# Weighting the expert rows on their way out of PSUM and adding them up in DRAM by the scatter, in a mixture-of-experts layer on one Trainium2 core

## The chip, the core and the metric

The kernel runs on one core of a Trainium2 chip. A core has a matrix engine (TensorE, PE in the profile), a vector engine (VectorE, DVE), an activation engine (ScalarE, ACT), a general one (GpSimd, POOL) and a sync engine (SyncE, SP) that here only issues transfers. Transfers run on 16 DMA engines, fed by queues; those that SP issues and those that POOL issues go through queues of their own. SBUF is the on-chip memory, PSUM the small memory into which TensorE writes, DRAM the device memory. The metric is the time of one launch in microseconds (us); less is better.

## The reference: what is computed

The input is 1024 latent tokens of 1024 float32 numbers and 256 context tokens. One layer is computed: modulation, input projection, two kinds of attention, output projection, and then the part that matters here, 32 experts of which each token takes four. Cut to that part:

```python
logits = t @ w_router + b_router
top_val, top_idx = lax.top_k(logits, TOP_K)        # TOP_K = 4
top_w = jax.nn.softmax(top_val, axis=-1)
# rows sorted by expert, in blocks of 128 with one expert each; empty places have weight 0
def expert_block(idx, e):
    hu = t[idx] @ w1[e] + b1[e]                    # 1024 -> 2048
    glu = jnp.minimum(hu[:, 0::2], 7.0)
    lin = jnp.clip(hu[:, 1::2], -7.0, 7.0)
    act = glu * jax.nn.sigmoid(1.702 * glu) * (lin + 1)
    return act @ w2[e] + b2[e]                     # 1024 -> 1024
y = y_rows * row_w[:, None]
out = jax.ops.segment_sum(y, row_tok, num_segments=1024)
x = x + ga2 * rmsnorm(out, g_post_ffn)
```

## The kernel before, in words

The program has five stages, each a block with a barrier behind it: `front` (modulation and projections), `attention`, `middle` (output projection, router, table of slots), `experts` and `combine`. Each engine has its own instruction list in each stage, written by hand, and they wait for each other by semaphores. Nothing reorders them.

**Attention** begins with transfers. SP loads `w_out` (two of 2 MB) into the ring, then a mask for head group A (`mask_a`), the bias of group B (two of 1.25 MB) and its mask (`mask_b`). POOL loads `sink` and copies the first queries (`queries`, L557). VectorE's first score needs `mask_a` and `sink` (L712). POOL adds `mask_b` to the bias (L570), and the heads of group B need the sum (`bias_ready`).

**Middle** ends with the router on VectorE: it picks four experts a token, computes `K.weights` (L995) and, for each of the 4096 choices, a slot number `K.slots`. Then POOL scatters 4096 records of two integers into `slot_d` (L855), 32 scatters. A record is (token, row of `y_d`), where choice k of a token has row `1024 k + token`. `slot_d` was filled in `front` with records of empty slots: token 0 and one of 128 spare rows of `y_d`.

**Experts** works in steps (`program`, L1146). A step is one expert with one block (single, R=1) or two blocks (pair, R=2) of 128 rows. The first loop runs a single step and a pair step alternately, 16 times each; the second runs 3 single steps. Together 35 steps and 51 blocks. A step has six units of weights, each 2 MB: four up (`UP`) and two down (`DOWN`). For each unit SP loads it into a ring of three (L1163), when VectorE and POOL have split the unit three before it (`lo_done`, `pool_lo_done`); ScalarE rounds it to its high part (L1256), VectorE (L1312, seven eighths) and POOL (L1208, one eighth, k = 7) form the low part, and TensorE does three products of each pair of tiles (L1402 to L1404).

POOL's list in a step (L1215 to L1243) also carries the rows:

- it copies the row numbers out of `record` to `y_row` (L1219), waits for that, and loads the next step's records (L1186);
- it splits unit 2, waits for the records, and gathers the next step's rows from `h2_d` into `xg` (L1190), one gather a block;
- it splits units 3, 4, 5 and the next step's 0;
- when ScalarE has copied the last result to `y` (L1296), it scatters `y` to `y_d` (L1239), one scatter a block, splits the next step's unit 1, and waits until the scatters have landed (L1242) before the next step begins.

TensorE transposes the gathered rows (`rows`, L1382) after its up units, and then the last activations (`columns`, L1389), before its down units.

**Combine** takes tiles of 128 tokens, eight in all. SP loads the four rows of each token (`yg`, 2 MB a tile) and the residual (`x1`, 0.5 MB), with two tiles of `yg` at a time; VectorE multiplies and adds the four rows (L1502, L1504), ScalarE takes the mean square (L1492), VectorE finishes (L1512 to L1516), and POOL stores the tile (L1483).

## Time and profile before

| | us |
|---|---|
| median of 3 runs | 3386.89 |
| lowest and highest of them | 3383.48, 3387.11 |
| the profiled execution's own time | 3385.55 |
| its span, first to last instruction | 3383.9 |

| engine | busy, us | share of the span |
|---|---|---|
| TensorE | 2891.7 | 85% |
| VectorE | 1887.1 | 56% |
| ScalarE | 1407.9 | 42% |
| GpSimd | 866.9 | 26% |

The stages lie one behind the other. The trace has the first instruction of `attention` at 453.0 us, the first of `experts` at 1262.1, and the first of `combine` at 3299.4, so `experts` is 60% of the span and `combine` 84.5 us. The DMA engines moved 629.36 MB, 444 MB of it expert weights. Busy time is an average over stages with different limits; the shares above do not say what bounds a stage.

### The profile page before, as it was taken

What the parts mean: (1) busy time and instruction counts of PE and PEld (TensorE: products, weight loads), DVE (VectorE), ACT (ScalarE), POOL (GpSimd) and SP (SyncE); (2) the same over time, 40 slices, a digit from 0 to 9 for tenths busy, and PEclk for the clock granted to TensorE, in tenths of its full rate; (3) what the DMA queues carried; (4) which work ended last, traced back from release to release, by engine and by line L of the source; (5) the groups of instructions that cost most, each with busy time, mean ns of one, the idle gap of its engine ahead of it and who ended that gap; (6) DMA issues with size and microseconds to landing.
All of it is one profiled execution on the core that took longest, in us unless ns stands there. A gap on an engine that the chain in (4) does not pass through costs nothing. (4 is left out here: it accounts for less than half of the span.)

```text
span 3383.9 us, 40318 instructions
## 1 busy us (share of the span) xinstructions
PE 2891.7 (85%) x13206; PEld 2182.2 (64%) x13207; DVE 1887.1 (56%) x2864; ACT 1407.9 (42%) x1667; POOL 866.9 (26%) x609
## 2 busy tenths in 40 slices
PE   4899989999957707999999999999999999999980
PEld 0254667777734406787787778777777777777760
DVE  0430024444422246767767776766677677767786
ACT  0100025555511105545545554555455445445551
POOL 1000021312111153223322422333233333323330
PEclk8999989999978858999999999999999999999995
DMA  9700032213132108667666765776676577667678
GB/s 242 254 25 25 13 93 68 68 45 86 45 105 87 62 18 306 239 217 260 238 221 242 269 232 211 263 269 213 234 261 247 207 265 254 229 219 276 241 281 310
DMA packets 285165, 629.36 MB, mean 186 GB/s; under 512 B 9922, under 2 KB 11202, under 8 KB 284962
## 3 DMA queue, kind: packets, MB, share of 16 engines
q1 hardware_dynamic: 261558, 549.12, 47.3%
q0 software_dynamic: 23568, 79.73, 6.6%
q8 instruction: 23, 0.38, 0.0%
q14 instruction: 16, 0.13, 0.0%
HBM read 584.63 MB, written 50.26 MB: 188 GB/s over the span
## 5 line engine op out<-in xcount | busy, mean ns | idle before, releaser
L1312 DVE TENSOR_TENSOR w_lo_x<-wring_x,w_hi_x 128x2048 fp32r<-128x2048 f32 (+1 forms) x422 | 874.0, 2115 | 195.8 <-PE psum L1404 191.5
L1256 ACT ACTIVATE w_hi_x<-wring_x 128x2048 fp32r<-128x2048 f32 x424 | 787.4, 1907 | 102.1 <-DMA wring_x<-in_w_mlp 101.8
L1402 PE MATMUL psum<-w_hi_x,x_hi_x 128*128 128x512 f32 x1632 | 676.6, 415 | 5.6 <-DVE w_lo_x L1312 5.6
L1403 PE MATMUL psum<-w_lo_x,x_hi_x 128*128 128x512 f32 x1632 | 637.2, 390 | 0.0
L1404 PE MATMUL psum<-w_hi_x,x_lo_x 128*128 128x512 f32 x1632 | 637.1, 390 | 0.0
L1208 POOL TENSOR_TENSOR w_lo_x<-wring_x,w_hi_x 128x512 fp32r<-128x512 f32 x212 | 327.8, 1550 | 888.3 <-PE psum L1404 810.5
L1402 PE MATMUL psum<-w_hi_x,a_hi_x 128*128 128x512 f32 x816 | 353.5, 433 | 0.0
L1402 PEld LDWEIGHTS psum<-w_hi_x,x_hi_x 128*128 128x128 f32 x1632 | 308.4, 189 | 65.9 <-DVE w_lo_x L1312 6.5
L1404 PEld LDWEIGHTS psum<-w_hi_x,x_lo_x 128*128 128x128 f32 x1632 | 306.9, 188 | 65.8
L1403 PEld LDWEIGHTS psum<-w_lo_x,x_hi_x 128*128 128x128 f32 x1632 | 307.6, 188 | 62.1
L1403 PE MATMUL psum<-w_lo_x,a_hi_x 128*128 128x512 f32 x816 | 329.9, 404 | 0.0
L1404 PE MATMUL psum<-w_hi_x,a_lo_x 128*128 128x512 f32 x816 | 327.6, 401 | 0.0
L1285 ACT ACTIVATE sig_x<-glu_x 128x256 f32<-128x256 f32 x204 | 84.9, 416 | 532.3 <-DVE glu_x L1356 532.1
L1356 DVE TENSOR_SCALAR glu_x<-psum 128x256 f32<-128x256 f32 x204 | 85.7, 420 | 270.5 <-PE psum L1404 270.2
L654 ACT ACTIVATE S<-S,negm 128x896 f32<-128x896 f32 (+1 forms) x128 | 119.6, 934 | 207.4 <-DVE negm L717 113.5
L465 PE MATMUL psum<-hT,ring 128*128 128x512 f32 (+1 forms) x496 | 200.9, 564 | 5.2 <-DVE hT L381 4.6
L630 PE MATMUL psum<-v,PT 128*128 (+1 forms) x1536 | 187.2, 273 | 0.0
L630 PEld LDWEIGHTS psum<-v,PT 128*128 128x128 f32 x1536 | 183.8, 194 | 0.0
L1404 PEld LDWEIGHTS psum<-w_hi_x,a_lo_x 128*128 128x128 f32 x816 | 160.7, 197 | 35.8
L1402 PEld LDWEIGHTS psum<-w_hi_x,a_hi_x 128*128 128x128 f32 x816 | 162.4, 199 | 32.9
L1403 PEld LDWEIGHTS psum<-w_lo_x,a_hi_x 128*128 128x128 f32 x816 | 161.6, 198 | 34.2
L1204 POOL TENSOR_TENSOR poolgate_x<-poolgate_x 128x1 f32<-128x1 f32 x70 | 96.0, 1372 | 341.7 <-ACT y_x L1296 246.0
(249 smaller groups left out, 3549.0 us busy)
## 6 DMA issues: line engine op xcount, KB each, us to landing
wring_x<-in_w_mlp SPq DMA_DIRECT2D x212, 2048.0 KB, 8.0
ring<-in_w_ada SPq DMA_DIRECT2D x12, 2048.0 KB, 9.0
bias<-bias_d SPq DMA_DIRECT2D x16, 1280.0 KB, 14.2
yg<-y_d SPq DMA_DIRECT2D x8, 2048.0 KB, 10.4
ring<-in_w_in SPq DMA_DIRECT2D x4, 2048.0 KB, 9.0
xin<-in_x SPq DMA_DIRECT2D x8, 512.0 KB, 5.1
ring<-in_w_out SPq DMA_DIRECT2D x2, 2048.0 KB
mix_d<-o SPq DMA_DIRECT2D x8, 512.0 KB, 6.6
```

Of the source, the lines that this page charges most:

```text
L465: last = pe.matmul(ps[:, g % 4, 0:width], lhs, rhs, start=(k == 0), stop=(k == KD - 1))
L630: last = pe.matmul(ps[:, 6 + s // NHA, head * HD:(head + 1) * HD], PT[:, s % 2, c * P:(c + 1) * P], v, start=(c == 0), stop=(c == chunks - 1))
L654: act.activation(S[:, s % 2, 0:keys(s)], S[:, s % 2, 0:keys(s)], ACT.Exp, bias=negm[:, s:s + 1], accum_out=den[:, s:s + 1]).then_inc(p_don ...
L1204: pool.tensor_tensor(poolgate[:, 1:2], poolgate[:, 0:1], poolgate[:, 0:1], ALU.add).then_inc(gate_open, 1)
L1208: pool.tensor_tensor(w_lo[:, n % LO, KP:, :], ring[:, n % RING, KP:, :], w_hi[:, n % HI, KP:, :].bitcast(F32), ALU.subtract).then_inc(pool ...
L1256: act.activation(w_hi[:, n % HI, k, :], ring[:, n % RING, k, :], ACT.Copy).then_inc(hi_done, 1)
L1285: act.activation(sig[:, j % 2, :], glu[:, j % 2, :], ACT.Sigmoid, scale=ALPHA).then_inc(sig_done, 1)
L1312: dve.tensor_tensor(w_lo[:, n % LO, k, :], ring[:, n % RING, k, :], w_hi[:, n % HI, k, :].bitcast(F32), ALU.subtract).then_inc(lo_done, 1)
L1356: dve.tensor_scalar(glu[:, s, :], pairs[:, :, 0], LIMIT, None, ALU.min).then_inc(glu_done, 1)
L1402: pe.matmul(bank, hi[:, r, k, :], w_hi[:, n % HI, k, :], start=False, stop=False)
L1403: pe.matmul(bank, hi[:, r, k, :], w_lo[:, n % LO, k, :], start=False, stop=False)
L1404: last = pe.matmul(bank, lo[:, r, k, :], w_hi[:, n % HI, k, :], start=False, stop=(k == KD - 1))
```

## The change

1. `y_d` has one row a token (1024) and 128 spare rows in place of 4096 and 128. Both it and 128 new spare rows of `h2_d` are filled with zeros by two transfers that POOL issues at the start of `attention`; POOL waits for them at that stage's end.
2. A record is now (token, weight as float32 bits). Four copies on VectorE put the weights into the records. Empty slots have a spare row as token and weight 0, so the gather of an empty slot reads a spare row of zeros in place of row 0.
3. In a step POOL copies the weights of the block to `y_weight` beside `y_row`, and the semaphore `gate_open` counts four a step in place of three. ScalarE's copy out of PSUM takes `y_weight` as its scale, and waits for it once a step.
4. The scatter adds: `compute_op=ALU.add`. Its row number is the token.
5. `combine` loads one row a token straight into `acc` (0.5 MB a tile), and the residual beside it, with three tiles in flight and buffers for all eight. The four multiplications and additions are gone.

```diff
-    record = np.stack(np.broadcast_arrays(token, token + SEQ * np.arange(TOPK)[None, :, None]), axis=-1)
+    record = np.stack([token, 0 * token], axis=-1)
...
-    spare = TOPK * SEQ + np.arange(SLOTS) % P
-    out["k_empty"] = np.stack([0 * spare, spare], axis=-1).astype(np.int32)
+    spare = SEQ + np.arange(SLOTS) % P
+    out["k_empty"] = np.stack([spare, 0 * spare], axis=-1).astype(np.int32)
...
-            self.h2_d = dram("h2_d", (SEQ, D))
+            self.h2_d = dram("h2_d", (SEQ + P, D))
...
-            self.y_d = dram("y_d", (TOPK * SEQ + P, D))
+            self.y_d = dram("y_d", (SEQ + P, D))
...
             pool.dma_start(sink[:, :], io["sink_a"].to_broadcast([P, NHA])).then_inc(sink_loaded, 16)
+            pool.dma_start(K.y_d, io["k_zeros"][0:1, 0:D].to_broadcast([SEQ + P, D])).then_inc(sums_zeroed, 16)
+            pool.dma_start(K.h2_d[SEQ:SEQ + P, :], io["k_zeros"][0:1, 0:D].to_broadcast([P, D])).then_inc(sums_zeroed, 16)
...
             pool.wait_ge(sink_loaded, 16)
+            pool.wait_ge(sums_zeroed, 32)
...
+            for k in range(TOPK):
+                link(dve.tensor_copy(record[:, k, :, 1].bitcast(F32), K.weights[:, :, k]))
...
-                pool.tensor_tensor(y_row[:, 0:st.R], record[:, 0:st.R, 1], int_zero[:, 0:st.R], ALU.add).then_inc(gate_open, 1)
-                pool.wait_ge(gate_open, 3 * st.passes + 3)
+                pool.tensor_tensor(y_row[:, 0:st.R], record[:, 0:st.R, 0], int_zero[:, 0:st.R], ALU.add).then_inc(gate_open, 1)
+                pool.tensor_copy(y_weight[:, 0:st.R], record[:, 0:st.R, 1].bitcast(F32)).then_inc(gate_open, 1)
+                pool.wait_ge(gate_open, 4 * st.passes + 4)
...
-                    pool.indirect_dma_start(K.y_d, bass.IndirectOffsetOnAxis(ap=y_row[:, r:r + 1], axis=0), y[:, r, :], None).then_inc(y_stored, 16)
+                    pool.indirect_dma_start(K.y_d, bass.IndirectOffsetOnAxis(ap=y_row[:, r:r + 1], axis=0), y[:, r, :], None, compute_op=ALU.add).then_inc(y_stored, 16)
...
+                        act.wait_ge(gate_open, 4 * st.passes + 4)
...
-                        act.activation(y[:, r, h * UNIT:(h + 1) * UNIT], ps[:, 4 + (h * st.R + r) % 2, :], ACT.Copy).then_inc(y_copied, 1)
+                        act.activation(y[:, r, h * UNIT:(h + 1) * UNIT], ps[:, 4 + (h * st.R + r) % 2, :], ACT.Copy, scale=y_weight[:, r:r + 1]).then_inc(y_copied, 1)
...
-                if t >= 2:
-
-                    sp.wait_ge(acc_done, t - 1)
-                sp.dma_start(yg[:, t % 2, :, :], y_rows[t]).then_inc(tile_loaded[t % 2], 16)
...
+                s = t % INFLIGHT
+                if t >= INFLIGHT:
+                    sp.wait_ge(tile_loaded[s], 32 * (t // INFLIGHT))
+                sp.dma_start(acc[:, t, :], K.y_d[t * P:(t + 1) * P, :]).then_inc(tile_loaded[s], 16)
+                sp.dma_start(x1[:, t, :], K.x1_d[t * P:(t + 1) * P, :]).then_inc(tile_loaded[s], 16)
```

Three places show how the instructions now stand. In the rows a bracket names the semaphores that an instruction waits for, and the numbers are the shape. First POOL at the start of `attention`, before and then after; `sink`, `y_d` and `h_d` are targets of transfers.

```order
L546 MEMSET zeros 128x256
L547 MEMSET qz 128x2048
L548 DMA sink<-in_sink_a 128x8
L557 COPY qz<-qaT 64x512 [waits tiles_loaded,zeros_set]
L557 COPY qz<-qaT 64x512
```

```order
L546 MEMSET zeros 128x256
L547 MEMSET qz 128x2048
L548 DMA sink<-in_sink_a 128x8
L549 DMA y_d<-in_k_zeros 1152x1024
L550 DMA h2_d<-in_k_zeros 128x1024
L559 COPY qz<-qaT 64x512 [waits tiles_loaded,zeros_set]
L559 COPY qz<-qaT 64x512
```

Two transfers of 1152 and 128 rows of 4 KB now stand between `sink` and the first queries. Second, POOL at the end of a pair step and the start of the single step behind it, before and after (`y_stored` counts landed scatters; the rows behind the line of dots are the start of the single step, which the loop runs next; unnamed rows, ISA and REGISTER_ALU, set registers or carry a wait).

```order
L1204 TENSOR_TENSOR poolgate_x<-poolgate_x 128x1 [waits y_copied_x]
L1239 DMA y_d<-y_x,y_row_x 4224x1024 x2
L1240 REGISTER_ALU
L1207 ISA [waits prod_done_x]
L1208 TENSOR_TENSOR w_lo_x<-wring_x,w_hi_x 128x512 [waits hi_done_x]
L1242 REGISTER_ALU
...
L1219 TENSOR_TENSOR y_row_x<-record_x,int_zero_x 128x1 [waits gate_open_x]
L1220 REGISTER_ALU
L1186 ISA [waits gate_open_x]
L1186 DMA record_x<-slot_d 128x2x2
```

```order
L1210 TENSOR_TENSOR poolgate_x<-poolgate_x 128x1 [waits y_copied_x]
L1246 DMA y_d<-y_x,y_row_x 1152x1024 x2
L1247 REGISTER_ALU
L1213 ISA [waits prod_done_x]
L1214 TENSOR_TENSOR w_lo_x<-wring_x,w_hi_x 128x512 [waits hi_done_x]
L1249 REGISTER_ALU
...
L1225 TENSOR_TENSOR y_row_x<-record_x,int_zero_x 128x1 [waits gate_open_x]
L1226 COPY y_weight_x<-record_x 128x1
L1227 REGISTER_ALU
L1192 ISA [waits gate_open_x]
L1192 DMA record_x<-slot_d 128x2x2
```

The order is the same; one copy stands ahead of the load of the records, and the two scatters now add. Third, SP in `combine`, first two tiles and the first that waits, before and after.

```order
L1470 DMA yg<-y_d 128x4x1024
L1474 DMA x1_rows<-x1_d 128x1024
L1470 DMA yg<-y_d 128x4x1024
L1474 DMA x1_rows<-x1_d 128x1024
L1470 DMA yg<-y_d 128x4x1024 [waits acc_done]
```

```order
L1476 DMA acc<-y_d 128x1024
L1477 DMA x1_rows<-x1_d 128x1024
L1476 DMA acc<-y_d 128x1024
L1477 DMA x1_rows<-x1_d 128x1024
L1476 DMA acc<-y_d 128x1024
L1477 DMA x1_rows<-x1_d 128x1024
L1476 DMA acc<-y_d 128x1024 [waits tile_loaded5_0]
```

The loads are a quarter of the size, and from the fourth tile on they wait for an earlier load in place of VectorE.

## Rows read from the trace of the kernel before

**Rows 1.** The page: busy time, share of the span, instructions of TensorE.

```profile
PE 2891.7 (85%) x13206; PEld 2182.2 (64%) x13207; DVE 1887.1 (56%) x2864; ACT 1407.9 (42%) x1667; POOL 866.9 (26%) x609
```

**Rows 2.** Last stage by window: stretch, length, busy times, TensorE clock, DMA share, GB/s.

```profile
3299.40:3369.40 70.00, 0.00 (x0) 0.00 (x0) 48.88 (x48) 11.39 (x22) 4.89 (x8) 0.50 0.96 359
```

**Rows 3.** Timeline, end of experts and last stage: start, length, engine, line [idle before].

```profile
3292.35 1.00 POOL L1239 DMA_INDIRECT y_d<-y_x,y_row_x  x1
...
3299.43 0.37 SPq L1470 DMA_DIRECT2D yg<-y_d  x1
...
3374.14 1.06 ACT L1492 ACTIVATE squares<-acc 128x1024 f32<-128x1024 f32 x1 [8.43 <-DVE acc L1504]
...
3379.71 0.53 POOL L1483 DMA_DIRECT2D out<-out_rows  x1 [2.12 <-DVE out_rows L1516]
```

**Rows 4.** Windows at the start of attention, columns as in rows 2.

```profile
453.00:463.00 10.00, 4.63 (x8) 2.52 (x8) 0.23 (x1) 1.28 (x1) 5.03 (x7) 0.66 0.78 220
463.00:470.70 7.70, 0.00 (x0) 0.00 (x0) 0.31 (x2) 0.00 (x0) 0.00 (x0) 0.63 1.06 363
470.70:483.30 12.60, 10.45 (x50) 8.59 (x51) 5.91 (x23) 5.25 (x11) 0.14 (x1) 0.68 0.95 198
```

**Rows 5.** Timeline at the start of attention: VectorE's first score, POOL's bias.

```profile
470.70 0.06 DVE L710 MEMSET gate<- 128x1 f32 x1 [7.33 <-DMA mask_a<-in_k_mask_a]
...
483.17 11.04 POOL L570 TENSOR_TENSOR bias<-bias,mask_b 128x5120 f32<-128x5120 f32 x1 [24.86 <-DMA mask_b<-in_k_mask_b]
```

**Rows 6.** DMA issues: the zero fill that front has, KB, us to landing.

```profile
skew_d<-in_k_zeros POOLq DMA_DIRECT2D x1, 2914.0 KB, 15.7
```

**Rows 7.** Timeline of VectorE in the router: a copy of 128x8 and the next.

```profile
1191.35 0.17 DVE L1015 COPY scan<-scan 128x8 f32<-128x8 f32 x1
1191.55 0.22 DVE L1016 TENSOR_TENSOR scan<-scan 128x56 f32<-128x56 f32 x1
```

**Rows 8.** Timeline of POOL from a pair step's scatters into a single step.

```profile
1996.22 2.33 POOL L1239 DMA_INDIRECT y_d<-y_x,y_row_x  x1 [0.16 <-issue]
1998.85 0.97 POOL L1239 DMA_INDIRECT y_d<-y_x,y_row_x  x1 [0.30 <-issue]
...
2002.94 1.22 POOL L1219 TENSOR_TENSOR y_row_x<-record_x,int_zero_x 128x1 int32<-128x1 int32 x1 [1.78 <-DMA y_d<-y_x,y_row_x]
2004.85 0.79 POOL L1186 DMA_DIRECT2D record_x<-slot_d  x1 [0.70 <-POOL y_row_x L1219]
...
2013.13 0.96 POOL L1190 DMA_INDIRECT xg_x<-h_d,record_x  x1 [0.30 <-issue]
2014.10 2.57 POOL L1208 TENSOR_TENSOR w_lo_x<-wring_x,w_hi_x 128x512 fp32r<-128x512 f32 x2
```

**Rows 9.** Timeline of TensorE: transposes of gathered rows (L1382), of last activations (L1389).

```profile
2018.69 1.09 PE L1382 MATMUL psum<-ident,xg_x 128*128 128x128 f32 x8 [1.24 <-DMA xg_x<-h_d,record_x]
2023.86 0.69 PE L1389 MATMUL psum<-ident,act_o_x 128*128 128x128 f32 x2 [4.08 <-DVE act_o_x L1361]
...
2252.84 1.10 PE L1382 MATMUL psum<-ident,xg_x 128*128 128x128 f32 x8 [1.67 <-DMA xg_x<-h_d,record_x]
...
2256.58 0.44 PE L1389 MATMUL psum<-ident,act_o_x 128*128 128x128 f32 x2 [2.64 <-DVE act_o_x L1361]
```

**Rows 10.** Windows of 1 us behind the two scatters, columns as in rows 2.

```profile
1999.00:2000.00 1.00, 1.00 (x6) 0.78 (x5) 0.73 (x2) 0.98 (x2) 0.98 (x2) 1.00 0.91 369
2000.00:2001.00 1.00, 1.00 (x6) 0.83 (x5) 0.97 (x2) 0.99 (x3) 1.00 (x1) 1.00 0.84 332
2001.00:2002.00 1.00, 1.00 (x6) 0.84 (x5) 0.97 (x3) 1.00 (x1) 0.15 (x1) 1.00 0.87 348
```

**Rows 11.** One line's instructions (L1219): ns min/median/max, first and last start.

```profile
L1219 POOL TENSOR_TENSOR y_row_x<-record_x,int_zero_x x35: 197/390/1699, 1288.9 to 3259.3; 128x1 int32<-128x1 int32 x19, 128x2 int32<-128x2 int32 x16
```

More of the change, by code:

```diff
@@ L1106, in experts @@
         record, y_row, int_zero = sb("record", [P, RMAX, 2], I32), sb("y_row", [P, RMAX], I32), sb("int_zero", [P, RMAX], I32)
+        y_weight = sb("y_weight", [P, RMAX])
         poolgate = sb("poolgate", [P, 2])
@@ L1457, in combine @@
         rows_loaded = sem("rows_loaded5")
-        tile_loaded = [sem("tile_loaded5_0"), sem("tile_loaded5_1")]
+        INFLIGHT = 3
+        tile_loaded = [sem(f"tile_loaded5_{t}") for t in range(INFLIGHT)]
         stored = [sem("stored5_0"), sem("stored5_1")]
-        acc_done, rms_done, out_done, dve_own, act_own = sem("acc_done"), sem("rms_done5"), sem("out_done"), sem("dve_own5"), sem("act_own5")
-        y_rows = K.y_d[0:TOPK * SEQ, :].rearrange("(k t p) d -> t p k d", t=T, p=P)
+        rms_done, out_done, dve_own, act_own = sem("rms_done5"), sem("out_done"), sem("dve_own5"), sem("act_own5")
         block = ctx.enter_context(nc.Block())
@@ L1497, in _ @@
             link = linker(dve, dve_own)
-            def add(t):
-                s = t % 2
-                dve.wait_ge(tile_loaded[s], 32 * (t // 2 + 1))
-                link(dve.tensor_scalar(acc[:, s, :], yg[:, s, 0, :], K.weights[:, t, 0:1], None, ALU.mult))
-                for k in range(1, TOPK):
-                    ins = dve.scalar_tensor_tensor(acc[:, s, :], yg[:, s, k, :], K.weights[:, t, k:k + 1], acc[:, s, :], ALU.mult, ALU.add)
-                    if k + 1 < TOPK:
-                        link(ins)
-                ins.then_inc(acc_done, 1)
-            def finish(t):
+            dve.wait_ge(rows_loaded, 32)
+            link(dve.tensor_tensor(gate2[:, :], gate2[:, :], gain[:, :], ALU.mult))
+            for t in range(T):
                 s = t % 2
```

33 lines of the change are left out of this document (11 added, 22 removed).

## The prediction, made before the changed kernel ran

> **What bounds the kernel now.** I read the page first, then windows of the three stages that the change touches, then the timeline of each. TensorE is busy 85% of the span [rows 1], nearly all of it in `experts`; that share says nothing of the other stages, so each is read by itself.
>
> The last stage is bound by transfers. Over its first 70 us the DMA engines are 0.96 busy at 359 GB/s, while VectorE works 48.88 of 70 us [rows 2]. The stage lasts from SP's first load at 3299.43 to the end of the span at 3383.9 [rows 3], 84.5 us.
>
> The start of `attention` is bound by transfers too. The DMA share is 0.78, 1.06 and 0.95 in the three stretches up to 483.3 [rows 4]. VectorE's first score waits for `mask_a` until 470.70, and POOL's addition to the bias waits for `mask_b` until 483.17 [rows 5]. The bias is not early: the addition ends at 494.2, about when the first head of group B comes up.
>
> In `experts` a pair step is TensorE's own: each weight unit serves two blocks and everything else has time. The single step behind a pair is the tight place, and there are 16 of them. There POOL's list is a chain: scatters, their landing, `y_row`, load of the records, gathers, splits [rows 8]. TensorE wants the gathered rows 1.24 us before they are there; they are transposed from 2018.69 on, and then TensorE stands for 4.08 us until 2023.86 for the last activations, which come from VectorE [rows 9]. So the chain on POOL is late already, but something else is later. The eight transposes take about 2.15 us, so the slack of the chain there is 2023.86 - 2018.69 - 2.15 = 3.0 us. The other step shown has 2256.58 - 2252.84 - 2.15 = 1.6. I formed it for all sixteen: 1.6 to 3.6, mean 2.84. This number decides the case.
>
> **The change part by part.**
>
> *The last stage.* It reads 8 x 0.524 MB of sums and as much of residual, 8.39 MB in place of 20.97, plus 1.05 MB for `gate2` and its gain as before. Work on VectorE falls to a reciprocal, a product and an addition a tile, below the time of a tile's transfers, and nothing waits for it. The last tile lands when the reads and about five of the eight stored tiles (2.62 MB) are through: 12.06 MB at 359 GB/s, the mean that includes the stage's start [rows 2], is 33.6 us. From the last square to the end of the span it is 3383.9 - 3374.14 = 9.8 us [rows 3]. Together 43.4, a gain of 41.1 us. Bounds: no store moves before the last tile lands (26.3 + 9.8 = 36.1, a gain of 48), or all do (38.0 + 9.8 = 47.8, a gain of 37).
>
> *The zero fill.* 1280 rows of 4 KB, 5.24 MB, start at about 456 us, in the stretch where the engines are full. SP's queue and POOL's share them, so both `mask_a` and `mask_b` get later; the fill ends before `mask_b` lands. At 363 GB/s [rows 4] the fill takes 14.4 us, and I take all of it as delay: after 483 the engines are idle, but the wait is over by then. Bounds: 0, if the fill is served behind SP's loads; 27.6, if it goes at the 190 GB/s of the other fill from the same zeros, 2.98 MB in 15.7 us [rows 6], and nothing beside it. That one shared the engines with weight loads, so I keep to 14.4. The two issues ahead of the first queries (about 0.6 us each) are hidden behind the wait for `mask_a`; without that cover they would cost 1.2.
>
> *Four copies in the router*, on the path to POOL's slot scatters. A linked copy of 128x8 takes 0.20 us start to start [rows 7]: +0.8.
>
> *ScalarE's scale and its wait.* A scale from a column in place of a constant; the wait is for a POOL instruction at the step's beginning, four units earlier. Nothing, hidden by those units; nobody waits behind it unless POOL's chain is 20 us late.
>
> *The adding scatter.* No row of before shows one. Two plain ones move 1.05 MB in the three windows from 1999 to 2002, and the share of the engines adds up to 0.91 + 0.84 + 0.87 = 2.6 us [rows 10]. Each row of `y_d` must now be read before it is written, so the engines read twice as much. I take the engine time doubled, +2.6 us at the second scatter's landing. Bounds: 0 (the reads from DRAM run beside those from SBUF), and +5.2 or more if a row is read, added and written without overlap. For the issue on POOL, 0.97 us free and 2.33 where it began beside VectorE [rows 8], I take +0.3 (0 to 1).
>
> A rule weighs on this term. The Trainium skill, Collectives: The Full Stack, section "The bandwidth ceiling: the fold count and why AG ≠ RS ≠ AR", says that an addition inside the DMA engines costs no cycles by itself but needs two source reads through one ring, so that the rate halves (it gives 1.93). No row here shows it; by it the sum would be the same as mine, since it names the doubling that I took as the middle.
>
> *`y_weight` on POOL.* It stands between `y_row` and the load of the records. `y_row` itself takes 0.197 us at least [rows 11], and 1.22 in the single step, where VectorE is splitting [rows 8]. I take 0.7, bounds 0.2 and 1.2. The 0.70 us between an instruction's end and the load that waits for it stays once.
>
> *The sum on the chain.* 2.6 + 0.3 + 0.7 = 3.6 us later in each single step behind a pair. Queued behind it on POOL are the record load, the split of unit 2, the gathers, the splits of 3 and 4. TensorE waits for the splits of 2 and 3 (the second comes 0.3 us before it is needed) and then for the gather, but the product of unit 3 is needed only at VectorE's next piece at about 2022, so a stall there is inside the slack. What is late next is the gathered rows: 3.6 - 2.84 = 0.76 us, sixteen times, 12.2 us. Bounds of the delay: 0.2 (no cost) to 7.4 (4.6 each, 73 us). The two single steps behind singles have one scatter, a delay of 1.3 + 0.3 + 0.7 = 2.3, below their slack of 2.6 and more: nothing. Pair steps have 11 us a unit: nothing.
>
> *The last scatter* has nobody to hide it: half of 2.6, +1.3, ahead of the barrier.
>
> *The sum*: -41.1 + 14.4 + 0.8 + 12.2 + 1.3 = -12.4 us. The profiled execution took 3385.55; the median of the runs is 1.3 above it, and I count from the median: 3374.5.
>
> **The rivals.**
>
> *Rival 1, the addition is free.* The chain gets 1 us later and stays under its slack. Then -41.1 + 14.4 + 0.8 = -25.9: 3361. For it: the engines are idle before 1999, and reads from DRAM and from SBUF come from different places. Against: both pass the same 16 engines, and 0.87 of them is taken while a scatter runs [rows 10].
>
> *Rival 2, the scatter's landing becomes the bound of the single steps.* Place: the wait for `y_stored` ahead of `y_row`. If the engine time grows by 5.2, the issue by 0.6 and the copy costs 1.2, the delay is 7.0, the cost 4.2 x 16 = 67 us, with 2.6 for the last scatter: -41.1 + 14.4 + 0.8 + 67 + 2.6 = +43.7: 3431. It turns the sign once the cost per step passes 24.6 / 16 = 1.5 us, a delay of 4.4, which is only 0.8 above my middle. For it: the weight load that SP issues at 2001.4 shares the engines with the second half of the scatters, and a stall of TensorE can lower its clock; in the first stretch of `attention` the granted clock is 0.66 [rows 4]. Against: up to 3 us are hidden in every step.
>
> *Rival 3, the fill goes at 190 GB/s* and holds up the loads for 27.6 us: +13.2 on the forecast, 3388, no change to be measured.
>
> **How the numbers follow.** Forecast 0.38, own range 3362 to 3388 (delay 3.0 to 4.6, stage gain 37 to 48); rival 1 0.22; rival 2 0.25, from 3394 up; rival 3 0.10; the rest, 0.05, a cost that I have not seen, on the slow side. The range that should hold it 8 times in 10 is 3358 to 3425. A difference of 0.2% (6.8 us) is about what a measurement of this kernel can tell from none. Faster by more: all of rival 1 and two thirds of the forecast, 0.46. Within: the rest of the forecast and half of rival 3, 0.20. Slower: 0.34.
>
> **What would show it.** The last stage 43 us long with the engines about full; the first score of `attention` at 482 to 485 and the bias at 497; windows behind two scatters with about 5.2 us of engine time; `y_row` 2.9 us later behind the scatters; TensorE's wait for the gathered rows about 5 in place of 1.2 us, and that for the last activations near 1. I am wrong if the landing moves by over 3.7 us, if the issue of an adding scatter takes much longer on POOL, or if the fill does not delay `mask_b`.

## The result, and the profile of the changed kernel

The changed kernel is slower. Its median is 3418.84 us (four runs, 3412.23 to 3421.43) against 3385.18 us for the kernel before; the ratio is 1.0108 with a 95% interval of 1.0082 to 1.0133, and the two medians lie 34 us apart. The prediction said 3374.5, faster by 11. The time lies inside the predicted range, and the sign is wrong.

The profiled execution took 3421.43 us, its span is 3419.6. Cut at the first load of records in `experts` and at SP's first load of the last stage, the two profiled spans compare like this:

| stretch | before | after | difference | predicted |
|---|---|---|---|---|
| up to `experts` | 1262.1 | 1287.3 | +25.2 | +15.2 |
| `experts` | 2037.3 | 2086.7 | +49.4 | +13.5 |
| last stage | 84.5 | 45.6 | -38.9 | -41.1 |
| span | 3383.9 | 3419.6 | +35.7 | -12.4 |

The gain came as forecast. Both costs came out larger, and the one in `experts` nearly four times as large.

**Attention.** These are the timeline rows that answer to [rows 5], and the fill's own row (KB, us from issue to landing):

```profile
492.24 0.06 DVE L713 MEMSET gate<- 128x1 f32 x1 [29.38 <-DMA mask_a<-in_k_mask_a]
...
505.77 11.05 POOL L572 TENSOR_TENSOR bias<-bias,mask_b 128x5120 f32<-128x5120 f32 x1 [46.00 <-DMA mask_b<-in_k_mask_b]
```

```profile
y_d<-in_k_zeros POOLq DMA_DIRECT2D x1, 4608.0 KB, 32.0
```

The first score starts 21.5 us later and the bias 22.6 us later. (The start of the bias differs by some us from one execution to the next: 500.9 to 506.0 us in the five traces with the fill at this place, 480.1 to 485.6 in the six of kernels without a fill.) The windows of the same stretch, columns as in [rows 2], show what the engines did meanwhile:

```profile
453.00:463.00 10.00, 4.26 (x8) 2.47 (x8) 0.54 (x2) 1.28 (x1) 6.32 (x9) 0.66 0.73 235
463.00:473.00 10.00, 0.00 (x0) 0.00 (x0) 0.00 (x0) 0.00 (x0) 0.00 (x0) 0.63 1.02 289
473.00:483.00 10.00, 0.00 (x0) 0.00 (x0) 0.00 (x0) 0.00 (x0) 0.00 (x0) 0.50 1.02 264
483.00:493.00 10.00, 0.00 (x0) 0.00 (x0) 0.76 (x2) 0.00 (x0) 0.00 (x0) 0.50 1.02 252
```

The engines are full, share 1.02, at 252 to 289 GB/s, where the loads alone ran at 363 [rows 4].

**Experts.** These rows are the same transition as [rows 8], the first two of [rows 9] and [rows 10], from a pair step's scatters into the single step behind it. The step's first product starts at 2029.7 here, and at 1993.4 before. First POOL, then SP and ScalarE, then TensorE:

```profile
2032.57 2.96 POOL L1246 DMA_INDIRECT y_d<-y_x,y_row_x  x1 [0.16 <-issue]
2035.84 1.56 POOL L1246 DMA_INDIRECT y_d<-y_x,y_row_x  x1 [0.30 <-issue]
2036.86 1.88 POOL L1214 TENSOR_TENSOR w_lo_x<-wring_x,w_hi_x 128x512 fp32r<-128x512 f32 x1
2043.31 0.19 POOL L1225 TENSOR_TENSOR y_row_x<-record_x,int_zero_x 128x1 int32<-128x1 int32 x1 [4.57 <-DMA y_d<-y_x,y_row_x]
2043.44 0.18 POOL L1226 COPY y_weight_x<-record_x 128x1 f32<-128x1 f32 x1
2044.34 0.81 POOL L1192 DMA_DIRECT2D record_x<-slot_d  x1 [0.72 <-POOL y_weight_x L1226]
```

```profile
2038.96 0.37 SPq L1169 DMA_DIRECT2D wring_x<-in_w_mlp  x1
```

```profile
2049.08 3.72 ACT L1263 ACTIVATE w_hi_x<-wring_x 128x2048 fp32r<-128x2048 f32 x2 [4.66 <-DMA wring_x<-in_w_mlp]
2052.70 0.40 ACT L1292 ACTIVATE sig_x<-glu_x 128x256 f32<-128x256 f32 x1
```

```profile
2058.01 1.09 PE L1390 MATMUL psum<-ident,xg_x 128*128 128x128 f32 x8 [1.88 <-DMA xg_x<-h_d,record_x]
2061.76 0.69 PE L1397 MATMUL psum<-ident,act_o_x 128*128 128x128 f32 x2 [2.65 <-DVE act_o_x L1369]
```

The second scatter's start to `y_row` takes 7.47 us, before it was 4.09 [rows 8]. Counted from the step's first product, the gathered rows are transposed at 28.3 us in place of 25.3. TensorE's wait in front of them has hardly grown, 1.88 for 1.24 us [rows 9]; over all sixteen steps the mean is 1.8 for 1.2. But the last activations, which I had taken to stand still, have moved too, from 30.5 to 32.0, and TensorE still stands for them when the rows are transposed: 2.65 us here and 2.8 on average, before 4.08 and 3.8. In none of the sixteen steps is this second wait shorter than 2.0 us, so the gathered rows never come last.

What the prediction did not look at is ScalarE. The same row of before, and the weight load behind it, are:

```profile
2001.37 0.37 SPq L1163 DMA_DIRECT2D wring_x<-in_w_mlp  x1
```

```profile
2009.69 3.72 ACT L1256 ACTIVATE w_hi_x<-wring_x 128x2048 fp32r<-128x2048 f32 x2 [2.86 <-DMA wring_x<-in_w_mlp]
```

This is the load of unit 4, the first `down` unit. SP issues it when its ring slot is free, that is, when POOL has split unit 1, and that split stands behind the two scatters on POOL. Before, it was issued 8.0 us into the step and was there at 16.3; after, 9.2 and 19.3. Behind its conversion ScalarE has the sigmoid of unit 2's activations; VectorE's product waits for that sigmoid, VectorE's split of unit 4 is queued behind the product, and behind the split come the activations of unit 3, for which TensorE waits. These are the three rows of VectorE, before and after: that product, the split of unit 4, and the first operation on unit 3's result.

```profile
2013.82 3.14 DVE L1361 TENSOR_TENSOR act_o_x<-lin_x,sig_x 128x256 f32<-128x256 f32 x1 [0.77 <-ACT sig_x L1285]
...
2017.21 5.01 DVE L1312 TENSOR_TENSOR w_lo_x<-wring_x,w_hi_x 128x2048 fp32r<-128x2048 f32 x2
2022.15 0.41 DVE L1356 TENSOR_SCALAR glu_x<-psum 128x256 f32<-128x256 f32 x1
```

```profile
2053.20 2.43 DVE L1369 TENSOR_TENSOR act_o_x<-lin_x,sig_x 128x256 f32<-128x256 f32 x1 [1.79 <-ACT sig_x L1292]
...
2055.89 3.94 DVE L1320 TENSOR_TENSOR w_lo_x<-wring_x,w_hi_x 128x2048 fp32r<-128x2048 f32 x2
2059.76 0.41 DVE L1364 TENSOR_SCALAR glu_x<-psum 128x256 f32<-128x256 f32 x1
```

The page's row for ScalarE's conversions tells the same of the whole span; these are the rows of before and of after, idle time before them last:

```profile
L1256 ACT ACTIVATE w_hi_x<-wring_x 128x2048 fp32r<-128x2048 f32 x424 | 787.4, 1907 | 102.1 <-DMA wring_x<-in_w_mlp 101.8
```

```profile
L1263 ACT ACTIVATE w_hi_x<-wring_x 128x2048 fp32r<-128x2048 f32 x424 | 787.3, 1907 | 156.1 <-DMA wring_x<-in_w_mlp 155.8
```

ScalarE waits 54 us more for weights. By the timelines of the sixteen single steps 2.1 us of it a step lie in front of unit 4 and 0.8 in front of unit 5. The windows behind the scatters show why the load lands late. Two scatters are 1.05 MB, as in [rows 10], but now they keep the engines full for twice as long, at about half the rate (the last two windows hold the beginning of the weight load too):

```profile
2036.00:2037.00 1.00, 1.00 (x6) 0.83 (x5) 0.97 (x3) 0.99 (x2) 1.00 (x2) 1.00 1.21 115
2037.00:2038.00 1.00, 1.00 (x6) 0.81 (x6) 1.00 (x1) 1.00 (x2) 1.00 (x2) 1.00 0.85 152
2038.00:2039.00 1.00, 1.00 (x6) 0.84 (x5) 1.00 (x1) 1.00 (x1) 0.74 (x1) 1.00 1.07 213
2039.00:2040.00 1.00, 1.00 (x7) 0.81 (x6) 0.97 (x3) 1.00 (x2) 0.00 (x0) 1.00 1.04 164
2040.00:2041.00 1.00, 1.00 (x6) 0.84 (x5) 1.00 (x1) 1.00 (x1) 0.00 (x0) 1.00 1.05 188
```

**The last stage**, as one window, and the wait that VectorE had in it:

```profile
3374.00:3404.00 30.00, 0.00 (x0) 0.00 (x0) 11.72 (x14) 12.68 (x25) 3.30 (x6) 0.50 0.98 381
3404.00:3419.60 15.60, 0.00 (x0) 0.00 (x0) 10.26 (x11) 0.15 (x1) 2.13 (x4) 0.50 0.35 142
```

```profile
3384.65 1.23 DVE L1502 TENSOR_TENSOR gate<-gate,gain 128x1024 f32<-128x1024 f32 x1 [23.17 <-DMA gain<-in_g_post_ffn]
```

The loads are through after 30 us, faster than I had reckoned. A tail of 15.6 us follows: VectorE could not start on the first tile until `gain` was there, 10.6 us into the stage, and then met stores that still held its two buffers (waits of 4.92, 2.46 and 0.55 us).

### The profile page after: what moved, and what is told of

It is laid out like the page before. It is cut to its first block and busy times, and to the rows that moved or that the text cites. A ratio compares the mean times of both kernels' runs of the same rounds, so it can differ in the third digit from the quotient of the medians.

```text
span 3419.6 us, 40371 instructions
## 1 busy us (share of the span) xinstructions
PE 2920.2 (85%) x13206; PEld 2187.4 (64%) x13207; DVE 1882.7 (55%) x2836; ACT 1417.0 (41%) x1667; POOL 866.8 (25%) x646
## 5 line engine op out<-in xcount | busy, mean ns | idle before, releaser
L1320 DVE TENSOR_TENSOR w_lo_x<-wring_x,w_hi_x 128x2048 fp32r<-128x2048 f32 (+1 forms) x422 | 883.0, 2136 | 194.6 <-PE psum L1412 190.8
L1214 POOL TENSOR_TENSOR w_lo_x<-wring_x,w_hi_x 128x512 fp32r<-128x512 f32 x212 | 351.6, 1663 | 888.0 <-PE psum L1412 782.3
## 6 DMA issues: line engine op xcount, KB each, us to landing
bias<-bias_d SPq DMA_DIRECT2D x16, 1280.0 KB, 14.1
```

What stands on the lines that cost most here:

```text
L1214: pool.tensor_tensor(w_lo[:, n % LO, KP:, :], ring[:, n % RING, KP:, :], w_hi[:, n % HI, KP:, :].bitcast(F32), ALU.subtract).then_inc(pool ...
L1320: dve.tensor_tensor(w_lo[:, n % LO, k, :], ring[:, n % RING, k, :], w_hi[:, n % HI, k, :].bitcast(F32), ALU.subtract).then_inc(lo_done, 1)
```

## The experiments

All were compared with the kernel before in the same session. Theory W is the one from the trace above: the late load of unit 4, through ScalarE and VectorE, sets the length of the single step. Rival L is the prediction's chain: landing, `y_row`, records, gather. The table at the end of this section has the steps side by side.

**e1, plain scatters.**

```diff
-  ... y[:, r, :], None, compute_op=ALU.add).then_inc(y_stored, 16)
+  ... y[:, r, :], None).then_inc(y_stored, 16)
```

> The changed kernel with plain scatters in place of adding ones: a row of the result holds one expert's part and not the sum, all else stays (the weight on leaving PSUM, the fill, the short last stage). The changed kernel takes 3418.8 us; its stage experts is 49.4 us longer than before. Theory (the addition itself makes experts longer: longer issue on POOL, later landing, more load on the DMA engines): nearly all of the 49 us comes back, what remains is the copy of the weight (0.2 us a step) and the later scale; experts within 4 us of before, about 3370 to 3374. Rival (the copy of the weight, the wait on ScalarE and the scale from a column, 689 in place of 600 ns, hold up the step): at least 15 us of the 49 stay, 3385 or more.

Measured: 3371.54 us, ratio 0.9977 (0.9967 to 0.9987). `experts` and the last stage together take 2085.0 us of the profiled span, 47.3 less than in the changed kernel. The single step is at 44.86 us, before 44.99. So the addition itself makes 47 of the 49 us, and the weight on leaving PSUM (689 in place of 600 ns an operation), its wait and the copy on POOL cost nothing that can be seen.

**e2, the fills behind SP's first loads.**

```diff
             load(0)
+            sp.dma_start(K.y_d, ...to_broadcast([SEQ + P, D])).then_inc(sums_zeroed, 16)
+            sp.dma_start(K.h2_d[SEQ:SEQ + P, :], ...).then_inc(sums_zeroed, 16)
             with sp.Fori(0, T - 1) as i:
```

> The changed kernel with the two zero fills issued by SP behind its first loads of attention (masks and bias of tile 0) in place of POOL ahead of them. Theory (the fill costs what it takes from these loads): POOL's first addition to the bias starts at 483 again in place of 505.8, the stage is 22.6 us shorter, about 3396. Rival (the fill costs the same wherever it runs in this stage, because the load of mask and bias of tile 1 then comes late in its place): VectorE waits for the second tile's mask, 3410 or more.

Measured: 3387.60 us, ratio 1.0028 (1.0013 to 1.0042). By the two ratios that is 27 us below the changed kernel; their intervals leave room for 22.6. The timeline has the bias where it was before the change:

```profile
481.93 11.06 POOL L573 TENSOR_TENSOR bias<-bias,mask_b 128x5120 f32<-128x5120 f32 x1 [24.98 <-DMA mask_b<-in_k_mask_b]
```

The fill itself takes longer there, 36.6 us to landing, and nobody waits for it. The bytes are the same; what cost was their place ahead of the loads that the stage waits for. (The edit also moves the fills from POOL's queue to SP's, and no run separates the place from the queue.)

**e3, POOL's split of unit 1 ahead of the scatters.**

```diff
+                pool.wait_ge(prod_done, units_done(st, NU))
+                split(unit + NU + 1, 1)
                 pool.wait_ge(y_copied, DOWN * (st.blocks + st.R) + 2)
                 gate()
                 (scatters)
-                pool.wait_ge(prod_done, units_done(st, NU))
-                split(unit + NU + 1, 1)
```

> The changed kernel with POOL's part of the split of the next step's unit 1 issued ahead of the scatters in place of behind them. Theory W (the single step is held up by the weight load of unit 4, which waits for this split and shares the DMA engines with the scatters): the load of unit 4 is issued 2 to 3 us earlier, ScalarE's wait for it falls from 4.6 to 2.5 us or less, and 1 to 2.7 us come back in each of 16 single steps: 3376 to 3403. Rival L (the single step is held up by the landing of the scatters, y_row, the records and the gather, as I predicted): the scatters start about 1 us later, so each of 16 single steps gets up to 1 us longer: 3419 to 3435.

Measured: 3527.30 us, ratio 1.0449 (1.0431 to 1.0466), by the two ratios 115 us above the changed kernel. Both theories missed it. In the same transition as above (first product at 2050.2):

```profile
2057.73 1.56 POOL L1248 DMA_INDIRECT y_d<-y_x,y_row_x  x1 [0.30 <-issue]
2069.87 0.18 POOL L1225 TENSOR_TENSOR y_row_x<-record_x,int_zero_x 128x1 int32<-128x1 int32 x1 [10.58 <-DMA y_d<-y_x,y_row_x]
...
2071.72 1.28 POOL L1214 TENSOR_TENSOR w_lo_x<-wring_x,w_hi_x 128x512 fp32r<-128x512 f32 x1
```

```profile
2073.06 0.79 PE L1410 MATMUL psum<-w_hi_x,x_hi_x 128*128 128x512 f32 x1 [6.08 <-POOL w_lo_x L1214]
```

The load of unit 4 was issued 5.6 us into the step, 3.6 earlier, as W said, and was still there only at 18.8. The scatters begin 2.8 us later than in the changed kernel, since POOL's split now stands ahead of them. With the load beside them from the start, the second one took 12.1 us from its start to `y_row` in place of 7.5. POOL's split of unit 2 is queued behind that wait, and TensorE stands 6 us for it inside unit 2's product. Whichever goes first, the load and the two adding scatters are both through only at about 19 us into the step. Behind the scatters hang POOL's splits, and they have little room too.

**e4, the landing off the chain.** The single step gets its own column of `y_row`, and POOL waits for `y_stored` behind the next gathers.

```diff
+                ycol = 0 if st.R == 2 else 2
-                pool.tensor_tensor(y_row[:, 0:st.R], ...
+                pool.tensor_tensor(y_row[:, ycol:ycol + st.R], ...
...
                 gather(next_r)
+                pool.wait_ge(y_stored, 16 * st.blocks + 16)
+                pool.sem_inc(y_free, 1)
...
-                pool.wait_ge(y_stored, 16 * (st.blocks + st.R))
-                pool.sem_inc(y_free, 1)
```

(An unused small load raises `y_stored` by 16 once at the start; the single steps behind singles keep their old wait.)

> The changed kernel with a column of y_row for the single step apart from the pair's, so that POOL waits for the landing of the scatters only behind the next gathers in place of ahead of y_row. Rival L (the landing is on the chain that holds up TensorE): the delay of about 3.4 us leaves the chain, and the 2.7 us a step come back: about 3375, or less. Theory W (the weight load of unit 4 holds it up): records and gathers come 5 us or more earlier and TensorE's wait for the gathered rows vanishes, but its wait for the last activations stays as long; the time changes by less than 10 us, 3409 to 3422.

Measured: 3409.49 us, ratio 1.0099 (1.0082 to 1.0116), where the changed kernel has 1.0108: not told apart. The mean single step is 0.7 us shorter. In this transition (first product at 2023.8) the load of the records is issued 10.2 us into the step in place of 14.6 and the first gather at 17.0 in place of 20.8. The issue is as early again as before the change (mean of the first gather 17.7, before 17.3). The rows themselves are not: they are transposed at 27.4 us on average, in the changed kernel at 28.3, before at 25.1, since the gathers now run beside the weight loads. ScalarE's conversion of unit 4 stays late, at 19.2:

```profile
2040.76 2.79 POOL L1196 DMA_INDIRECT xg_x<-h_d,record_x  x1 [0.52 <-issue]
```

```profile
2042.98 3.72 ACT L1266 ACTIVATE w_hi_x<-wring_x 128x2048 fp32r<-128x2048 f32 x2 [3.40 <-DMA wring_x<-in_w_mlp]
```

L said that 2.7 us a step come back, and TensorE would stop waiting for the rows; neither came. By itself this run leaves open what rows as early as before would have given. That they are not what costs follows with the wait behind them: in each of the sixteen steps, here as in the changed kernel, TensorE stands for the last activations after the rows are transposed (2.9 us on average, 1.8 at least).

**e5 and e6, bytes that nobody waits for, in the kernel before.** After e3 a broader theory stood beside W: the engines are full in that stretch, and each byte in it is paid (theory D). SP loads 1.05 MB more into a buffer of its own, behind unit 4's load, in each single step (e5) or in each pair step (e6).

```diff
                     load(st, n, e)
+                    if n == 4 and st.R == 1 and st.s is st.p:       # e6: st.R == 2
+                        sp.dma_start(extra[:, :, :], K.x1_d[0:2 * P, :]...).then_inc(extra_loaded, 16)
```

> The kernel before, with one more transfer that nobody uses: in each single step of the first loop SP loads 256 rows of x1_d (1.05 MB) into a buffer of its own, behind the weight load of unit 4; POOL's list is untouched. In the trace the DMA engines are full from 8 us behind the start of a single step (the first weight load) to 36 us. Theory D (the single step behind a pair is bound by the engine time of all transfers in that stretch, so the adding scatter costs what it takes from the engines and not what its landing delays): 1.05 MB at about 400 GB/s is 2.6 us, 16 times, plus 42 us, ratio to before 1.010 to 1.014. Rival (only the chains on POOL count, landing, y_row, records, splits): none of them is touched, ratio within 0.003 of 1.

> The same as the run before it, with the same 1.05 MB in each pair step (behind the load of unit 4) in place of the single step. Theory D: a pair step takes 72 us for the same six weight loads, the engines have idle time in it, and the transfer costs nothing, ratio 0.998 to 1.002. Rival (a transfer more costs its engine time wherever it runs): as much as in the single step, 1.010 to 1.014.

Measured: e5 3387.62 us, ratio 1.0019 (1.0007 to 1.0031); e6 3378.69 us, 0.9997 (0.9987 to 1.0007). Theory D falls: 1.05 MB behind unit 4's load costs 0.26 us a step and not 2.6. ScalarE's wait for unit 5 grows from 1.2 to 5.0 us in this transition, and that is nearly all covered.

**e8, the rows of empty slots left out of gathers and scatters**, on the changed kernel, by an index out of bounds.

```diff
-    spare = SEQ + np.arange(SLOTS) % P
+    spare = 4 * SEQ + np.arange(SLOTS) % P
...
-  ... compute_op=ALU.add)
+  ... compute_op=ALU.add, bounds_check=SEQ - 1, oob_is_err=False)     # the gathers too
```

> The changed kernel with the empty slots' indices beyond the last row and a bound on the indices of gathers and scatters, so that the rows of empty slots (6528 slots for 4096 expert rows, 37%) are neither read nor added. Theory D (engine time counts): of the two adding scatters and the two gathers in the stretch, some 7.8 us of engine time, about a third goes, 2 to 3 us in each of 16 steps, 3370 to 3390. Rival (the price lies in the issue and in the waits, not in the bytes): the issue takes as long as before, 3410 to 3420.

Measured: 3411.68 us, ratio 1.0098 (1.0071 to 1.0126). The software queue moves 1.11 MB in the transition that I read in place of 2.10, with windows in which the engines are only 0.4 to 0.5 busy, and yet unit 4's load is there at 19.7 us into the step and the mean single step is 47.40. Over the sixteen steps 1.41 MB are left of 2.07. So a third fewer bytes (in the transition shown half) and the same time; theory D had 2 to 3 us less a step. A guess that I did not test: the rows that stay lie on some of the sixteen engines, and a transfer lands with its slowest engine.

**e9, the same bytes as e5, just ahead of unit 4's load.**

```diff
+                    if n == 4 and st.R == 1 and st.s is st.p:
+                        (the waits for the split of unit 1)
+                        sp.dma_start(extra[:, :, :], K.x1_d[0:2 * P, :]...).then_inc(extra_loaded, 16)
                     load(st, n, e)
```

> The kernel before with the same unused 1.05 MB load as in e5, in the same single steps, but just ahead of the weight load of unit 4 in place of just behind it (it waits for the same splits). Behind it, it cost 0.2 us a step. Theory W (what counts is when the load of unit 4 lands, since ScalarE waits for it at 16 us into the step, and the activations and TensorE behind that): it lands 2.6 us later, and the step gets 1.5 to 2.6 us longer, ratio to before 1.007 to 1.013. Rival (the waiting of ScalarE for that load is covered by VectorE's own list, and what the change cost came another way): ratio within 0.003 of 1.

Measured: 3415.23 us, ratio 1.0089 (1.0061 to 1.0116), 30 us or 1.9 a step by the ratio; the single steps in the trace are 1.4 longer. POOL's list is as in the kernel before, `y_row` starts 1.8 us behind the split as there, and the conversion of unit 4 begins 2.9 us later on average:

```profile
2014.32 3.72 ACT L1266 ACTIVATE w_hi_x<-wring_x 128x2048 fp32r<-128x2048 f32 x2 [5.54 <-DMA wring_x<-in_w_mlp]
```

e5 and e9 differ by the order of two issues 0.5 us apart. This is the case of the changed kernel without an adding scatter in it. It delays more than unit 4, though: unit 5's load stands behind it in the same queue, and its conversion starts at 25.9 us in place of 21.9 (26.0 in the changed kernel). In 11 of the 16 steps here the last activations wait for the sigmoid that ScalarE has behind unit 5's conversion. So e9 shows that late weight loads make the step longer, and not how much of that is unit 4's.

**e10, the split of unit 1 later by 1.1 us, without bytes**, in the kernel before.

```diff
                 pool.wait_ge(prod_done, units_done(st, NU))
+                if st.R == 2:
+                    pool.tensor_tensor(idle[:, :], ..., ALU.add)        # 128x512, read by nobody
                 split(unit + NU + 1, 1)
```

> The kernel before with one more operation of POOL (an addition of 128x512 on a buffer that nobody reads, about 1.3 us) between the second scatter of a pair step and the split of unit 1. It moves no bytes; the wait of 3 us for the landing in front of y_row takes it up, so records and gathers stay where they are. Theory W: the load of unit 4 is issued 1.2 us later and the step gets as much longer at most, 0.8 to 1.2 us by sixteen, ratio 1.003 to 1.006. Rival (only the bytes that share the engines count, not the time of the issue): ratio within 0.002 of 1.

Measured: 3393.10 us, ratio 1.0022 (1.0006 to 1.0039), 7.5 us, 0.5 a step. SP issues unit 4's load at 9.0 us in place of 8.0, ScalarE has it at 16.85 in place of 16.11. W is right in sign, and I had the size too large: about half of the delay reaches the end of the step. The run is no clean one: the added operation also holds up VectorE's product beside it (2.38 us for 1.38), POOL's load of the records (1.0 later) and the gathered rows (26.2 for 25.1 us on average), which I had expected to stay.

**e7, e11 and e12, the pair's scatters moved.** A third buffer of `y` and 256 spare rows in place of 128; the two scatters of a pair step are issued in the following single step, behind the split of unit 5. e7 is the changed kernel with this and with e2's fills, e11 the kernel before with this alone, e12 is e7 with plain scatters.

```diff
-        y = sb("y", [P, RMAX, D])
+        y = sb("y", [P, 3, D])
...
                 for n in range(3, NU):
                     pool.wait_ge(prod_done, units_done(st, n - 1))
                     split(unit + n, n)
+                if st.R == 1 and st.s is st.p:
+                    pair_scatter()                                      # y[:, 0:2], then_inc(pair_stored, 16)
...
+                if st.R == 1:
+                    pool.wait_ge(pair_stored, 32 * st.p + 32)
                 gate()
-                for r in range(st.R):
+                if st.R == 1:
                     (scatter of y[:, 2])
```

> The changed kernel with the fills behind SP's first loads (e2) and a third buffer of y: the two adding scatters of a pair step are issued behind the split of unit 5 of the following single step, in place of ahead of it, and the records and gathers no longer wait for their landing. Theory D: 1.05 MB of adding scatters (about 5 us of engine time) leave the full stretch of each of 16 single steps; besides the 2.7 us that the change cost there, part of the time comes back that TensorE stood for the activations before the change too, 3 to 5 us a step: 50 to 80 us less than e2's 3388, 3308 to 3338. Rival (the engines stay full there, and the scatters only collide with the loads of unit 5 and of the next step): 3370 to 3390.

> The kernel before, with nothing of the change, and with the pair's scatters issued behind the split of unit 5 of the following single step, as in e7. In e7 a single step takes 43.5 us from its first product to the next one's, in the kernel before 45.0, in the changed kernel 47.6. If the deferral gives the same without the change (the adding scatter costs nothing there), 1.5 us or a little more come back sixteen times: 3345 to 3358, ratio 0.989 to 0.993. If e7's gain hung on the changed last stage alone, the ratio is 1.000.

> e7 with plain scatters in place of adding ones; a row of the result holds one expert's part and not the sum. It prices the addition where its landing has 13 us to come. If the addition is free there: the same as e7, ratio 0.982 to 0.985. If the engines in the second half of the step are the bound: 1 to 2.6 us a step less, 16 to 42 us, ratio 0.971 to 0.979.

Measured: e7 3327.31 us, ratio 0.9835 (0.9814 to 0.9855); e11 3371.54, 0.9953 (0.9940 to 0.9966); e12 3331.21, 0.9844 (0.9816 to 0.9871). In e7 the load of unit 4 is issued at 5.7 us into the step with nothing of the scatters beside it, and ScalarE converts it at 13.7 without a wait (here; 14.1 on average). The adding scatters go out behind all that, and e12 shows that the addition then costs nothing. e11 gains 1.25 us a step by the trace (43.74 for 44.99), and e7 has 1.5; e11's ratio is a miss, 0.989 to 0.993 was expected. e7 lies in the range that theory D had named, which e5 had already excluded: W and D agree where the scatters are moved away from the load. e7 beats the kernel before by 1.65%. Its profiled span is 55.0 us shorter: 39.2 in the last stage, 13.3 in `experts` and 2.4 ahead of it. The sixteen single steps give 24.6 us. Of these 11 are lost again elsewhere in `experts`: 4.0 from the last scatter to the last stage (which adds here too), 3.3 in the two last single steps, 2.8 ahead of the first step, the rest in the first and the pair steps. That is one execution of each, and the two last steps differ by about as much between other kernels.

The table has means over the 16 single steps that follow a pair, from the timelines, in us from the step's first product (the first with `btab_x`): the start of unit 3's products, the start of ScalarE's conversion of unit 4, the start of unit 4's products, and the first product of the next step.

| kernel | unit 3 | conversion of unit 4 | unit 4 | next step |
|---|---|---|---|---|
| before | 17.51 | 16.11 | 30.58 | 44.99 |
| after | 18.05 | 19.49 | 33.10 | 47.59 |
| e1 plain scatters | 17.52 | 15.92 | 30.66 | 44.86 |
| e3 split first | 24.78 | 18.98 | 39.33 | 53.79 |
| e4 landing off the chain | 17.84 | 19.28 | 32.53 | 46.85 |
| e5 extra behind unit 4 | 17.51 | 16.11 | 31.07 | 45.25 |
| e8 empty rows left out | 17.89 | 19.49 | 33.19 | 47.40 |
| e9 extra ahead of unit 4 | 17.51 | 18.96 | 32.03 | 46.38 |
| e10 split later | 17.57 | 16.85 | 30.94 | 45.33 |
| e11 before, deferred | 17.51 | 14.15 | 29.78 | 43.74 |
| e7 deferred | 17.52 | 14.09 | 29.05 | 43.46 |
| e12 deferred, plain scatters | 17.51 | 13.90 | 29.03 | 43.44 |

By e9 a conversion of unit 4 later by 2.85 us goes with a step longer by 1.39, by e10 0.74 with 0.34; the changed kernel has 3.38 and 2.60. How the 2.60 come about can be followed in the means of its sixteen steps. The conversion of unit 4 starts 3.38 us later, VectorE's product behind the sigmoid 3.24 (23.60 for 20.36), its split of unit 4 2.81 (26.19 for 23.38), its first operation on unit 3's result 1.73 (30.05 for 28.32), the last transposes 2.49 (32.62 for 30.13), the next step 2.60. The delay shrinks on the way because that product and that split together took 1.5 us longer before than after. It grows again at the end because in three of the sixteen steps unit 5's load is so late that the sigmoid behind its conversion comes last:

```profile
2537.37 3.71 ACT L1263 ACTIVATE w_hi_x<-wring_x 128x2048 fp32r<-128x2048 f32 x2 [4.98 <-DMA wring_x<-in_w_mlp]
2540.98 0.40 ACT L1292 ACTIVATE sig_x<-glu_x 128x256 f32<-128x256 f32 x1
...
2542.82 0.69 PE L1397 MATMUL psum<-ident,act_o_x 128*128 128x128 f32 x2 [2.60 <-DVE act_o_x L1369]
```

Those three steps take 49.5 to 50.0 us. In two of them TensorE waits 3.6 and 4.1 us for the gathered rows first, but even there it then stands 2.6 us for the activations.

TensorE itself is late too in unit 3: it starts 0.54 us later, and inside it waits for VectorE's and POOL's splits (0.7 and 0.4 us in most of the sixteen), which it did not before. This is covered: it has done all that stands ahead of the gathered rows at 26.5 us (before 24.0), and VectorE comes to unit 3's result only at 30.05. This is a reading of one trace; no run separates the part of unit 4 from that of unit 5, or from the time that POOL's instructions take from VectorE.

## Why the prediction was wrong, point by point

*The last stage* was right: -38.9 against -41.1, inside -48 to -37. Its parts were less so. The transfers took 30 us for my 33.6, and the tail 15.6 for 9.8, since I had nothing waiting for VectorE, and it waited for `gain` first.

*The fill* had the right mechanism and place; both masks got later, and nothing absorbed it. The term is mis-sized: 14.4 for a measured 22.6. I turned bytes into time by the 363 GB/s of loads into SBUF, where the profile held another fill from the same zeros at 190 [rows 6]; I set that aside because weight loads ran beside it. The 5.24 MB in 22.6 us make 232 GB/s, between the two. Rival 3's bound of 27.6 was the nearer end. With e2 the cost is gone at once, so the term was also one that a place behind the loads would have taken away.

*The four copies in the router* are right: the trace has them 0.2 us apart, 0.17 each. The rest of 25.2 - 22.6 = 2.6 us is no more than executions differ by up to `experts`.

*ScalarE's scale, its wait and `y_weight`* were right at nothing. `y_weight` takes 0.18 us, and `y_row` fell from 1.22 to 0.19, because it starts later now, when VectorE is not splitting.

*The adding scatter's own price* was right in kind and somewhat low. The five windows above hold 5.2 us of engine time where two plain ones took 2.6 [rows 10]; by the packets of POOL's queue it is 6.3 for 2.6 on average, +3.7 for my +2.6. Where the scatters are moved, a packet of 4 KB takes 332 ns with the addition (e7) and 159 without (e12), 2.1 times. The Trainium skill, Collectives: The Full Stack, section "The bandwidth ceiling: the fold count and why AG ≠ RS ≠ AR", has 1.93 for an addition in a ring collective. No run here is a collective, but the doubling agrees. The issue grew by 0.6 for my 0.3, and the second landing came 4.1 us later against the step's start, beyond the 3.7 that I had named as a sign of being wrong. That the record load is only 3.2 us later, for my 3.6, is luck in part: `y_row` got 1.0 shorter. The gathered rows are 3.2 later too.

*What that delay costs* is the step that failed. The prediction says "What is late next is the gathered rows: 3.6 - 2.84 = 0.76 us, sixteen times, 12.2 us." The slack of 2.84 was the distance to the last activations, and it was misread to begin with: I took 2.15 us for the eight transposes, whose row says 1.09 [rows 9]. TensorE's own wait for the activations, 4.08 and 2.64 us in the two steps shown and 3.8 on average, is the slack. With it the chain that I priced costs nothing, and the 12.2 us of the sum vanish; it then gives -24.6 us, next to rival 1. The larger error is in what the slack means. It was only slack if the last activations stood still, and they came 2.5 us later. They hang on VectorE and ScalarE, those on the loads of units 4 and 5, and the load of unit 4 on the same scatters twice over: it is issued behind POOL's split, which stands behind their issue, and it shares the engines with them. I had both in hand. The split was in my list of POOL's chain, and I named the weight load at 2001.4 that shares the engines, but only as something that speaks for rival 2. e4, which takes the landing off my chain, gives back 0.7 us a step of 2.6; e9, which delays only weight loads, costs 1.4 by the trace and 1.9 by the ratio. The sum had +12.2 us here, and the sixteen steps took 41.6.

That a stall of TensorE in unit 3 "is inside the slack" was right, as said above. For *the last scatter* I gave 1.3; from its issue to the last stage it takes 10.9 us in place of 7.1, so 3.8. Pair steps, held at nothing, take 0.1 us more each, and the two single steps behind singles 2.4 together, about what these two differ by between other kernels.

*The rivals.* Rival 1, the addition is free, is excluded by e1 as long as the scatters stand where they do, and e12 shows it true where they are moved. Rival 2 had the side right and the mechanism wrong: it put the bound at the wait for `y_stored`, which e4 took off the chain. Its break-even, 1.5 us a step, was sound, and the measured 2.6 is beyond it. Of the signs that I had named, the fill's was to be 482 to 485 for the first score (492.2), TensorE's wait for the gathered rows "about 5" (1.8 on average) and for the last activations "near 1" (2.8); the last two by themselves show the wrong chain. The bias was to start at 497 and started at 505.8.

## What to carry to other kernels

A slack between two arrivals is worth its face value only if the later one does not hang on the thing that you delay; follow that one back to its own transfers first. Here a transfer that got heavier cost little by its landing and most by the loads that stand next to it: look for the first load behind it that an engine waits for, and move one or the other, before giving up on the change. Bytes for which nobody waits soon belong behind the loads of the stage in which they are issued.

## What the hardware showed

- One and the same unused load of 1.05 MB in a single step made that step 1.4 us longer in the trace when issued just ahead of the critical load and 0.3 just behind it (e9 and e5; by the ratios 1.9 and 0.4), and cost nothing in a pair step (e6, ratio 0.9997).
- The fill from DRAM to DRAM kept the DMA engines at a share of 1.02 with 252 to 289 GB/s together with the loads, against 363 for the loads alone, and took 32.0 us for 4.7 MB.
- A packet of 4 KB of a scatter took a DMA engine 332 ns with the addition (e7) and 159 ns without (e12).
- A weight load beside two adding scatters took 10.1 us from issue to ScalarE when issued behind them, and 13.2 us (e3) when issued ahead of them; it was through at about 19 us into the step both times.
- The issue of an adding scatter on POOL took 1.56 us for 0.97 and 2.96 for 2.33, and VectorE's product of 128x256 beside that issue and POOL's next split 2.6 us for 1.4, on average over the sixteen steps.
- Leaving out the rows of empty slots took a third of the bytes off POOL's queue (2.07 to 1.41 MB a transition) and did not bring the next load forward: 19.49 us into the step both times (e8).
